# Five norms move into the projection blocks that follow them; rows are normalized in halves, PSUM is read straight into high and low parts, the root's table is loaded a block ahead

## The reference, cut to what matters

```python
def rms_norm(x, g):
    y = xf * lax.rsqrt(jnp.mean(xf * xf, axis=-1, keepdims=True) + RMS_EPS)
    return (y * g).astype(x.dtype)
def layer_norm(x, g, b):
    ...
    y = xc * lax.rsqrt(var + LN_EPS) * g + b
# first stack
h = h + mixer(rms_norm(h, norm_mix[i]));  h = h + conv_ffn(rms_norm(h, norm_ffn[i]), ...)
# second stack
h = layer_norm(alpha * h + mix, ...)
h = layer_norm(alpha * h + memory_cross_attention(h, ...), ...)
h = layer_norm(alpha * h + hierarchical_moe(h, ...), ...)
```

## Time and profile before

| what | value |
|---|---|
| time, median of 3 runs | 2006.76 us (2004.83 to 2009.04) |
| the profiled execution, its own time | 2012.14 us |
| its span | 2010.3 us |
| PE busy | 1856.8 us (92%) |
| PEld busy | 1442.2 us (72%) |
| DVE busy | 940.0 us (47%) |
| ACT busy | 728.7 us (36%) |
| mean granted clock of TensorE | 0.964 |
| HBM, mean over the span | 185 GB/s |

### The profile page before, as it was taken

The page is one execution under the profiler, slowest core; times in us unless marked ns, Lnnn a source line. Parts: engine busy times, 40 slices in busy tenths (PEclk is TensorE's granted clock), DMA queues, the critical chain, the costliest instruction groups (busy, mean ns, idle before and its releaser), DMA issues. The chain is left out here.

```text
span 2010.3 us, 31309 instructions
## 1 busy us (share of the span) xinstructions
PE 1856.8 (92%) x13202; PEld 1442.2 (72%) x13202; DVE 940.0 (47%) x1860; ACT 728.7 (36%) x1348; POOL 0.2 (0%) x4
## 2 busy tenths in 40 slices
PE   7998999999999679998999898999988899999996
PEld 5777999785799579997887787555545678755553
DVE  5575565511766545556466656110123665611002
ACT  4464444203343344444455444211112354421111
POOL 0000000000000000000000000000000000000000
PEclk9999999999898789999999999999998999899998
DMA  7503444243000324433351234899982133389993
GB/s 287 209 1 126 175 184 160 92 157 130 23 3 3 136 94 189 189 147 126 130 205 43 105 126 151 350 426 424 424 326 83 43 105 132 145 361 425 425 424 165
DMA packets 33841, 374.39 MB, mean 186 GB/s; under 512 B 4880, under 2 KB 6032, under 8 KB 9120
## 3 DMA queue, kind: packets, MB, share of 16 engines
q1 hardware_dynamic: 30544, 363.89, 45.4%
q10 hardware_dynamic: 3152, 8.42, 1.2%
HBM read 371.25 MB, written 1.05 MB: 185 GB/s over the span
## 5 line engine op out<-in xcount | busy, mean ns | idle before, releaser
L1738 PE MATMUL ps<-ring,arena 128*64 128x256 f32 x2048 | 235.1, 382 | 0.0
L144 PE MATMUL ps<-ident 128*128 128x256 f32 x714 | 188.3, 408 | 40.2 <-PEq L501 7.5
L427 PE MATMUL ps<-ffn_x_h,ffn_w_h 128*128 128x256 f32 x704 | 202.5, 288 | 15.5 <-DVE ffn_w_l L422 15.5
L422 DVE TENSOR_TENSOR w_l<-ring,w_h 128x512 fp32r<-128x512 f32 x256 | 171.3, 689 | 85.7 <-ACT w_h L419 84.3
L419 ACT CAST w_h<-ring 128x512 fp32r<-128x512 f32 x256 | 156.2, 620 | 140.9 <-PE ps L427 140.4
L427 PE MATMUL ps<-ffn_x_l,ffn_w_h 128*128 128x256 f32 x704 | 202.1, 287 | 0.0
L427 PE MATMUL ps<-ffn_x_h,ffn_w_l 128*128 128x256 f32 x704 | 202.0, 287 | 0.0
L1738 PEld LDWEIGHTS ps<-ring,arena 128*64 128x64 f32 x2048 | 141.4, 137 | 69.1
L144 PEld LDWEIGHTS ps<-ident 128*128 128x128 f32 x714 | 137.9, 203 | 71.3 <-issue 53.7
L427 PE MATMUL ps<-w_h,x_h 128*128 128x512 f32 x416 | 163.7, 393 | 5.4 <-DVE w_l L422 5.4
L422 DVE TENSOR_TENSOR ffn_w_l<-ring,ffn_w_h 128x1024 fp32r<-128x1024 f32 x132 | 155.2, 1220 | 18.7 <-ACT ffn_w_h L419 18.7
(11 more groups left out here) (331 smaller groups left out, 2984.3 us busy)
## 6 DMA issues: line engine op xcount, KB each, us to landing
ring<-in_w_moe SPq DMA_DIRECT2D x64, 2048.0 KB, 10.9
ring<-in_w_proj SPq DMA_DIRECT2D x38, 2048.0 KB, 8.1
ring<-in_w_ffn SPq DMA_DIRECT2D x22, 3072.0 KB, 10.1
ring<-in_w_moe SPq DMA_DIRECT2D x64, 1024.0 KB, 11.1
rows<-in_ln_g ACTq DMA_DIRECT2D x6, 512.0 KB, 4.1
rows<-in_ln_b ACTq DMA_DIRECT2D x6, 512.0 KB, 5.4
ring<-in_w_lora SPq DMA_DIRECT2D x1, 2560.0 KB, 8.8
ring<-in_w_b_in SPq DMA_DIRECT2D x1, 2496.0 KB, 9.7
```

Source lines behind the costliest of these rows:

```text
L144: pe.matmul(bank(b)[:, 0:2 * P].rearrange("p (o f) -> p o f", o=2), ident[:], wide, start=True, stop=True, skip_group_check=True)
L422: return dve.tensor_tensor(low, x, high.bitcast(F32), ALU.subtract)
L427: last = pe.matmul(out, a[x], b[y], start=start and n == 0, stop=stop and n == 2, skip_group_check=True)
L1738: last = pe.matmul(bank(0)[g * SLOTS_E:(g + 1) * SLOTS_E, 0:2 * P], x[:, k, e * SLOTS_E:(e + 1) * SLOTS_E], wg[:, g, k, :], start=(k == 0) ...
```

## The change

Five norms lose their block and open the one behind: those ahead of the first projection, of both FFN stages and of both cross-attentions. There ScalarE splits the first weight chunk, then does the norm; VectorE does the norm, then its part of the first chunk. Rows are scaled in halves of 512, transposes go half by half (features 0 to 3 of both row tiles, then 4 to 7), into one PSUM place of 128x256 for each feature tile. From there ScalarE makes the high part with the gain and VectorE the low part; with a bias (LayerNorm) ScalarE writes `xT` first and both split from there. Signals go out for each feature tile (4 to 7 together). Fillers are 3 ahead of the transposes and 2 behind them (4 in the FFN).

The five norms that keep a block (`rwkv`, the final norm of the first stack, those ahead of both mixtures and that behind the first mixture) also use halves and whole feature tiles; four are evacuated by each engine, gain and bias in one VectorE instruction, with 3 fillers ahead and 4 behind. The last norm (`norm_out`) centres and multiplies by the gain row in one instruction, scales and adds the bias row in another, all on VectorE, and stores row tile 1 in two halves. The root's table is asked for (`load_root`) at the end of ScalarE's list in the block before. The six `ahead` transfers are issued at unit 1 of the FFN.

```diff
+        def norm_dve(dve, norm):
...
+            for c in row_halves():
...
+                    ins = dve.tensor_scalar(norm.src[:, 0, c], h[:, 0, c], rstd[:, 0:1], None, ALU.mult)
+                ins.then_inc(ready.up(), 1)
...
+        def norm_pe(pe, norm, place, after):
+
+            ready, tp = [sig("normed_dve"), sig("normed_act")], sig("transposed")
+            for f in range(2):
+                for t in range(T):
+                    pe.wait_ge(ready[t].sem, ready[t].at(f + 1))
+                    for k in range(4 * f, 4 * f + 4):
+                        ins = pe.transpose(place(k)[:, t * P:(t + 1) * P], norm.src[:, t, k * P:(k + 1) * P], ident[:])
+                        if t == T - 1 and k in after:
+                            ins.then_inc(tp.up(after[k]), after[k])
+        def split_place(k):
+            return bank(2 + k)[:, 0:SEQ] if k < 6 else bank(k)[:, SEQ:2 * SEQ]
+        SPLIT_AFTER = {0: 1, 1: 1, 2: 1, 3: 1, 7: 4}
...
+        def norm_x_act(act, norm, xs, k):
+
+            tp, made, high, split = sig("transposed"), sig("x_made"), sig("x_high"), sig("x_split")
+            if norm.kind == "ln":
+                for m in ((0, 1) if k == 0 else (k + 1,)):
+                    if m < KD:
+                        act.wait_ge(tp.sem, tp.at(split_turned(m)))
+                        act.activation(xT[:, m, :], split_place(m), ACT.Identity, bias=norm.bias[:, m:m + 1], scale=norm.gain[:, m:m + 1]).then_inc(made.up(), 1)
+                act.wait_ge(made.sem, made.at(k + 1))
+                act.copy(xs[0][:, k, :], xT[:, k, :]).then_inc(high.up(), 1)
+                return
+            act.wait_ge(tp.sem, tp.at(split_turned(k)))
+            if k >= 6:
+                act.wait_ge(split.sem, split.at(k - 1))
+            act.activation(xs[0][:, k, :], split_place(k), ACT.Copy, scale=norm.gain[:, k:k + 1]).then_inc(high.up(), 1)
...
+                if norm is not None:
+                    if norm.first:
+                        load_root(act)
+                    split_weights(0)
+                    norm_act(act, norm)
...
-                    fill(pe, 5)
+                    if norm is None:
+                        fill(pe, 5)
+                    else:
+                        fill(pe, 3, 0)
+                        norm_pe(pe, norm, split_place, SPLIT_AFTER)
+                        fill(pe, 2, 0)
...
+                    if residual is not None and u == units - 1:
+                        load_root(act)
...
-                        for o, x in ahead:
-                            act.dma_start(o, x).then_inc(ahead_in.up(16), 16)
-                        split_act(act, xs[0], xT[:], x_high)
...
+                        split_chunk(0, 0)
+                        norm_act(act, norm)
+                        for k in range(KD):
+                            norm_x_act(act, norm, xs, k)
...
+                            if u == 1:
+                                for o, x in ahead:
+                                    act.dma_start(o, x).then_inc(ahead_in.up(16), 16)
```

More of the change, by code:

```diff
@@ new lines, in norm_act @@
+        def norm_act(act, norm):
+            ms_ready, root, inv_ready, ready = sig("mean_square"), sig("row_root"), sig("inverse_ready"), sig("normed_act")
+            act.wait_ge(ms_ready.sem, ms_ready.at(1))
+            act.activation(std, ms, ACT.Sqrt).then_inc(root.up(), 1)
+            act.wait_ge(inv_ready.sem, inv_ready.at(1))
+            for c in row_halves():
+                if norm.kind == "ln":
+                    ins = act.activation(h[:, 1, c], h[:, 1, c], ACT.Identity, bias=shift[:, 1:2], scale=rstd[:, 1:2])
+                else:
+                    ins = act.activation(norm.src[:, 1, c], h[:, 1, c], ACT.Copy, scale=rstd[:, 1:2])
+                ins.then_inc(ready.up(), 1)
@@ L271, in norm, with split_norm, place @@
+        def split_norm(kind, gain, bias=None, z=None, first=False):
+            if kind == "ln":
+                unscaled.append(bias is not None)
+            return Norm(kind, gain, bias, z if kind == "rms" else h, first)
+        def norm(kind, gain, bias=None, z=None):
+            norm = Norm(kind, gain, bias, z if kind == "rms" else h, False)
+            def place(k):
+                return bank(k // 2)[:, (k % 2) * SEQ:(k % 2 + 1) * SEQ]
             with new_block() as block:
-                ms_ready, root, inv_ready = sig("mean_square"), sig("row_root"), sig("inverse_ready")
@@ new lines, in _ @@
+                @block.vector
+                def _(dve):
+                    norm_dve(dve, norm)
+                    for k in (2, 3, 6, 7):
+                        dve.wait_ge(tp.sem, tp.at((k | 1) + 1))
+                        if bias is None:
+                            dve.tensor_scalar(xT[:, k, :], place(k), gain[:, k:k + 1], None, ALU.mult)
+                        else:
+                            dve.tensor_scalar(xT[:, k, :], place(k), gain[:, k:k + 1], bias[:, k:k + 1], ALU.mult, ALU.add)
@@ new lines, in _, with norm_out @@
+                @block.tensor
+                def _(pe):
+                    fill(pe, 3)
+                    norm_pe(pe, norm, place, {1: 2, 3: 2, 5: 2, 7: 2})
+                    fill(pe, 4)
+            if kind != "rms":
+                unscaled.append(bias is not None)
+        def norm_out(store):
+            with new_block() as block:
+                ms_ready, root, inv_ready, rows_in, done = sig("mean_square"), sig("row_root"), sig("inverse_ready"), sig("rows_loaded"), sig("rows_done")
+                centred = sig("centred")
+                @block.scalar
+                def _(act):
@@ L287, in _ @@
[L287 to L295, removed]
@@ L319, in _ @@
[L319 to L325, removed]
@@ L326, in _ @@
[L326 to L333, removed]
@@ L346, in _ @@
[L346 to L356, removed]
@@ L458, in _, with split_weights @@
             def _(act):
[L459 to L463, removed]
+                def split_weights(q):
                     if q % KD == 0:
```

211 lines of the change are left out of this document (136 added, 75 removed).

## The result

The changed kernel takes 1978.47 us (median of 4 runs, 1976.43 to 1984.82) against 2007.03 (median of 4, 2004.83 to 2009.04): ratio 0.9863, 95% interval 0.9839 to 0.9888, 28.6 us less. Forecast were 31.1 less and 1975.7. The profile before was one of its slower executions (2012.14 against a median of 2007.03), so the medians, and not the two spans, give the size of the gain.

A forecast was written before the change was run, and what follows sets the result against it. The prediction took the bound to be the serial norm chains between one block's last product and the next block's first. Its terms summed to 31.1 us saved, median 2006.8 to 1975.7, range 1967 to 1989.

The forecast's parts named there:

- the forecast case: Whole kernel: the summed savings come as priced, 31.1 us less, median 1975.7; chance 0.69, own range 1968 to 1982.
- first attention: First norm, opening the first projection: Sqrt waits for the weight split, first product at 18.4 instead of 20.44; saves 2.0 us.
- FFN 0: Fused opening of FFN 0: first product at 174.0 instead of 180.62, no low clock behind it; saves 7.5 us.
- FFN 1: Fused opening of FFN 1: 10.6 us saved there, less the cost of transfers moved to unit 1; net 6.8.
- last norm: Final norm_out: centring under the root, two passes per row tile instead of three, smaller last transfer; saves 2.3 us.
- the exposed transfers: FFN 1: six transfers issued at unit 1 delay the chunk's cast by 3.4 us; TensorE gap 3.63 becomes 7.0.
- Cross-attention: Both cross-attention openings: first product earlier (1153.9 instead of 1157.74 at cross 0), rest shifts rigidly; saves 3.6 and 4.4 us.
- The table: Hoisting the root's table load at eight norms: 0.83 us saved at each LayerNorm, 0.64 at an RMS norm.
- Norms ahead of the experts: Two norms keeping their block before the mixtures: table, half rows and even evacuation save 1.3 us each.
- The clock: Rival, chance 0.15: fewer fillers let the clock fall in four warm openings, 2.8 us each; 20 saved, 1987.
- The handshake case: Rival, chance 0.08: ScalarE and VectorE pieces do not overlap, each split opening loses 3 us; 16 saved, 1991.
- stall behind table loads: Rival, chance 0.01: a further 1.3 us stall goes with the load at eight places; 10 us more, 1965.

The follow-up runs named there:

- all_four: Changed kernel with one table load after the branches, FFN 1 transfers in unit 0, cross-attention scalings spread, first norm before the weight split: 1967.89 us, ratio 0.9808.
- table_only: Kernel before, with only the root's table loaded a block ahead, behind the mixtures after the branches join: 1997.87 us, ratio 0.9960.
- no_fillers: Changed kernel without any filler in the five fused openings; executed once, read by stages: FFN 0 +1.0 us, both cross-attentions 0.0.
- lead_only: Kernel with the four repairs, without the fillers behind the transposes in the five fused openings; read by stages: FFN 0 took 204.82 us.

## Why the prediction was right, and where not

**The sum.** 31.1 us were forecast, 28.6 came, within the range; the forecast case was the one that happened. Taken by the stages that repeat, both pairs of profiles give: first attention 2.5 and 2.0 (2.0 forecast), FFN 0 7.6 twice (7.5), FFN 1 8.1 and 7.3 (6.8), cross 1 3.3 twice (4.4), last norm 2.5 twice (2.3). The nearness of the total is in part luck. What can be traced is about 25 us: 2.0 at the first projection (from the program's start 2.3 and 1.7), 7.6, 7.7, 2.4 or 1.0 at cross 0, 3.3, 2.5, 0.55 each at RWKV's norm and at the final norm of the first stack, with 0.7 lost in the experts (means of both pairs, an estimate from the stages). The other 3 of the 28.6 lie in stages that differ by as much between two profiles of one kernel.

**FFN 0 and 1** held step by step: root 0.2 late behind the weight cast (0.3 forecast), low parts at 0.4 a piece where I took 0.45, no low clock in the opening. In FFN 1 the exposed transfers cost 2.7 at unit 1, not 3.4. ScalarE and its queue ahead of unit 1, after:

```profile
708.49 0.62 ACT L510 CAST ffn_hid_h<-arena 128x512 fp32r<-128x512 f32 x1 [2.98 <-DVE arena L1039]
708.50 0.39 ACTq L978 DMA_DIRECT2D arena<-in_mem  x1
...
711.14 0.45 ACTq L978 DMA_DIRECT2D arena<-in_lam  x1
711.69 3.88 ACT L510 CAST ffn_w_h<-ring 128x1024 fp32r<-128x1024 f32 x4 [2.58 <-issue]
```

The issuing takes 3.1 us, and 0.6 of it runs beside the cast of the hidden values that was given out just before; ScalarE stands idle for the other 2.58. That is 0.7 of the term's surplus of 0.5 to 1.3.

**The first norm** was priced right in its unusual part: the added wait for ring unit 0 held the Sqrt until 12.99 (12.95 forecast), and undoing it gave 1.5.

**Cross-attention, the step that failed.** The first product came where I put it (about 4.4 us behind the block's start). I let the rest of the stage shift rigidly. But within the stage VectorE scales the rows of `h`, four instructions. Cross 0, the first product and the first pair of scalings after, and that pair before:

```profile
1127.39 0.38 PE L518 MATMUL ps<-x_h,w_h 128*128 128x256 f32 x1
```
```profile
1136.14 2.35 DVE L262 TENSOR_TENSOR h<-h,rows 128x1024 f32<-128x1024 f32 x2
```
```profile
1165.12 2.35 DVE L258 TENSOR_TENSOR h<-h,rows 128x1024 f32<-128x1024 f32 x2
```

Counted from the block's start (1122.97 after, 1149.51 before) the first product moved from 8.2 to 4.4, by 3.8; the scaling from 15.6 to 13.2, by 2.4, and its four instructions occupy VectorE for some 4.8 us. The gap at chunk 8 went from 1.07 to 2.34, 1.3 us given back, which is the 1.1 missing at each. all_four took the gap away and the stage gave back 2.6. The longer gap has a second price: in one of the two profiles the clock fell behind it in cross 0, for 1.5 us more.

**The table.** Its size was right (table_only), its reach was not: I counted eight places, but at the two behind a mixture the load stayed, since it was put inside a branch. At the last norm that cost nothing (all_four gained 0.0), because the centring covers it. At the norm of latent attention none of the forecast 0.6 came; taking the second load away did not bring it either, as TensorE's slow fillers hold the transposes back anyway (all_four); table_only gained nothing there either. There I had counted a gain on VectorE's chain that TensorE does not let through.

**Norms ahead of the experts.** Inside the block the forecast 1.3 came: from its start (1234.5 and 1205.6) to the first transfer of the mixture it took 7.0 us before and 5.7 after. The stages did not pass it on: experts 0 lost 0.8 and 0.1, experts 1 0.3 both times. In the 21 us of routing that follow, TensorE's mean clock was lower in the first pair of profiles (stretch; length, then busy time and records of PE, PEld, DVE, ACT and POOL, clock, DMA share, GB/s), before and after:

```profile
1241.00:1262.00 21.00, 18.85 (x116) 15.91 (x118) 14.14 (x49) 7.22 (x11) 0.00 (x0) 0.84 0.04 9
```
```profile
1212.00:1233.00 21.00, 18.39 (x106) 15.70 (x107) 13.19 (x48) 6.51 (x11) 0.00 (x0) 0.76 0.04 9
```

That does not explain it. In the second pair the clock of this stretch was 0.76 before and 0.84 after, the other way round, and the stage gained nothing either; in experts 1 it was 0.76 before and 0.84 after in both pairs. Over the eleven profiles the first product of an expert comes 22.2 to 26.0 us after the norm's start, so a gain of 1.3 in front of it cannot be told from that. What sets the length of the routing is open.

**The rivals.** The clock did not fall in the openings. Without any filler it did in three of the four warm ones (no_fillers), and with the three leading ones alone it stayed up in FFN 0 (lead_only). The handshake case is out: 0.40 to 0.44 a piece. No stall behind table loads.

## What to carry to other kernels

When a chain is shortened at the front of a stage, look for the next thing on each engine's list that is not tied to the first product: here 4.8 us of row scaling on VectorE took back a third of the gain, and spreading it between chunks returned twice that. A table asked for inside a branch was loaded again after the join; asked for behind the branch it was loaded once (here without a gain, as other waits covered it). Compare stages between anchors that both kernels have: the total of one profile swings by up to 12 us, while FFN 0, cross 1 and the last norm repeat within 0.1.

## What the runs showed of the hardware that was not expected

The granted clock of RWKV, a stage with many short waits, differs from run to run of the same program: 0.84 or 0.89 over 150 us of it, 7 to 9 us of time. How long TensorE was without work did not alone decide whether the clock fell: 2.89 us were followed by 1.2 GHz in FFN 0 without fillers, 2.63 us in cross 0 were not, and the same gap of 2.34 us in cross 0 was followed by it in one execution of the changed kernel and not in the other. A few extra fillers that left 2.85 us empty did not prevent the fall, they moved the point at which it came.
